# A hybrid MLA and RWKV-7 layer on one core: chunk decay factors by way of DRAM, a sum of squares in another place, down sums in another order

## What is computed

```python
def step(S, inp):
    r_t, w_t, k_t, v_t, kk_t, a_t = inp
    sa = jnp.einsum('bhvk,bhk->bhv', S, -kk_t)
    S = (S * w_t[:, :, None, :] + sa[..., None] * (kk_t * a_t)[:, :, None, :]
         + v_t[..., None] * k_t[:, :, None, :])
    return S, jnp.einsum('bhvk,bhk->bhv', S, r_t)
```

## Time and profile before

| | us |
|---|---|
| median of 3 runs | 1897.72 |
| lowest and highest | 1897.05, 1898.7 |
| the profiled execution, its time | 1898.8 |
| the profiled execution, its span in the profile | 1897.0 |
| PE busy (share of the span) | 1795.9 (95%) |
| DVE, POOL, ACT busy | 955.3, 691.5, 384.9 |
| mean granted clock of TensorE (1 is full speed) | 0.976 |

### The profile page before, as it was taken

How to read it: one execution, slowest core, us unless ns; L and a number is a source line. 1 busy time by engine, 2 the same in 40 slices (tenths; PEclk the granted TensorE clock), 3 DMA queues, 4 the chain that set the end, 5 groups by cost and what they waited for, 6 DMA issues and landing times. The chain is left out here.

```text
span 1897.0 us, 34197 instructions
## 1 busy us (share of the span) xinstructions
PE 1795.9 (95%) x14597; PEld 1336.5 (70%) x14597; DVE 955.3 (50%) x1710; ACT 384.9 (20%) x918; POOL 691.5 (36%) x495
## 2 busy tenths in 40 slices
PE   5999999999997987999899899999999999899998
PEld 3566666666665664555566788888888888688887
DVE  2757767766776773555333543343444334324422
ACT  2333333334333322333100111100001000000000
POOL 2553664555354534445320111222222220534522
PEclk9999999999997888999999999999999999999999
DMA  9343244324221006110130211101111112233331
GB/s 377 111 152 103 77 136 135 94 88 157 92 80 54 7 7 163 46 45 1 75 128 9 105 45 45 35 32 45 45 45 45 45 45 73 84 114 115 122 101 64
DMA packets 70906, 158.62 MB, mean 84 GB/s; under 512 B 19290, under 2 KB 47786, under 8 KB 66531
## 3 DMA queue, kind: packets, MB, share of 16 engines
q1 hardware_dynamic: 66866, 115.74, 19.0%
q10 hardware_dynamic: 3888, 40.70, 6.0%
HBM read 128.30 MB, written 20.44 MB: 78 GB/s over the span
## 5 line engine op out<-in xcount | busy, mean ns | idle before, releaser
L2337 PE MATMUL psum<-mixT,wA 128*128 128x264 f32 x1408 | 337.3, 388 | 1.9 <-DVE rb L2579 1.5
L2337 PEld LDWEIGHTS psum<-mixT,wA 128*128 128x128 f32 x1408 | 268.3, 191 | 48.6 <-DVE rb L2579 1.7
L2337 PE MATMUL psum<-u_sum,wA 128*128 128x264 f32 x1232 | 297.4, 386 | 0.5 <-DVE u_sum L2562 0.5
L437 PE MATMUL psum<-wsl,xt 128*128 128x368 f32 (+1 forms) x1092 | 283.8, 452 | 8.8 <-DMA wsl<-in_w_in 5.7
L2337 PEld LDWEIGHTS psum<-u_sum,wA 128*128 128x128 f32 x1232 | 234.3, 190 | 41.1 <-issue 0.9
L437 PEld LDWEIGHTS psum<-wsl,xt 128*128 128x128 f32 (+1 forms) x1092 | 150.0, 172 | 90.8 <-issue 18.1
L2492 POOL TENSOR_TENSOR wA<-wA 128x512 f32<-128x512 f32 x22 | 28.6, 1299 | 427.6 <-DMA wA<-in_w_gate 233.4
L2337 PE MATMUL psum<-hid,wA 128*128 128x264 f32 x528 | 121.6, 386 | 2.1 <-DVE hid L2630 1.5
L2337 PEld LDWEIGHTS psum<-hid,wA 128*128 128x128 f32 x528 | 100.2, 190 | 19.9 <-issue 2.8
L2505 POOL TENSOR_TENSOR u_sum<-wA 128x1280 f32<-128x1280 f32 x8 | 24.7, 3092 | 184.6 <-DMA wA<-in_w_down 184.6
L2337 PE MATMUL psum<-mixT,u_sum 128*128 128x264 f32 x352 | 82.9, 392 | 9.4 <-POOL u_sum L2511 9.4
(11 more groups left out here) (362 smaller groups left out, 2875.9 us busy)
## 6 DMA issues: line engine op xcount, KB each, us to landing
wsl<-in_w_in ACTq DMA_DIRECT2D x27, 1472.0 KB, 6.9
wA<-in_w_down SPq DMA_DIRECT2D x32, 704.0 KB, 4.1
wA<-in_w_gate SPq DMA_DIRECT2D x22, 512.0 KB, 4.4
wA<-in_w_up SPq DMA_DIRECT2D x22, 512.0 KB, 4.4
mixed<-proj SPq DMA_DIRECT2D x8, 784.0 KB
xt<-in_x_tiles SPq DMA_DIRECT2D x9, 512.0 KB, 6.0
wsl<-in_w_in SPq DMA_DIRECT2D x3, 1472.0 KB, 11.3
out_y<-hid SPq DMA_DIRECT2D x1, 4224.0 KB, 12.0
```

What stands on the lines that cost most here:

```text
L437: return pe.matmul(out, lhsT, rhs, start=start, stop=stop)
L2337: ins = pe.matmul(pb[bank][:, 0:NW], left(k), right(k), start=first and k == 0, stop=k == depth - 1, skip_group_check=not first)
```

## The change

Three parts.

1. The four products of two columns are gone, and with them ACT's exponential of `ends` and the wait for `qts_ok` ahead of them. The exponential of the running sum is now written to `grown`, which is the buffer of `sig`; POOL's product with it goes to rR. Rows 63 and 127 of `grown` are the factors of the two chunks. SP stores these two rows (2 x 2 KB) to spare rows of the scratch tensor `v` in DRAM, at the end of a step, after a wait for `rR_e`; at the start of the next step it waits for that store (`pc_st`) and loads them into `pc`, 128 x 8, of single elements of 4 bytes with channels on the partitions (`pc_in`). `pc` now has column 4c + j. `state_out` waits for `pc_in`, and the next tile's first write to `sig` waits for `pc_st` and for POOL's `R_ok`. `transposes_x` waits for `kts_ok` and `qts_ok` itself.
2. On PE `ssq(t+3)` goes behind `state_close(t,1)`, on DVE `row_mean(t+3)` behind `state_out(t,1)`.
3. In the down products POOL forms S3 first, then S2 = A22 - S3, then S1 = S2 + A11, and waits for `a22_in` only ahead of S2. DVE forms T3, T2 = T3 + B11, T1 = B22 - T2. PE runs Z ahead of Y and W. SP's waits follow the new last readers.

```diff
@@ -172,6 +172,7 @@
     keff = sb("keff", [P, RW])
+    grown = sig
     rR = sb("rR", [P, RW])
@@ -255,6 +256,7 @@
     v_rows = io.v.rearrange("t p h d -> (t p) h d")
+    ends = io.v.rearrange("t p h d -> (t p) (h d)")[KEYS:KEYS + 2 * TILES]
     ident = c_("ident")
@@ -318,7 +320,7 @@
     def decay_sums(f):
-        return (pb[4], pb[6]) if f else (pb[1], pb[2])
+        return pb[4] if f else pb[1]
 
@@ -383,6 +385,12 @@
             f = t + 1
+            if t >= 0:
+                sp.wait_ge(s["pc_st"], 16 * f)
+                if t >= 2:
+                    sp.wait_ge(s["S_ok"], 2 * t - 2)
+                sp.dma_start(pc[t % 2][:, :], ends[2 * t:2 * t + 2].rearrange("c (j p) -> p (c j)", p=P),
+                             allow_slow_non_contiguous=True).then_inc(s["pc_in"], 16)
             if f < TILES:
@@ -415,6 +423,8 @@
                     sp.dma_start(io.qT[:, :, (f - 1) * P:f * P], qts).then_inc(s["st_kv"], 16)
+                sp.wait_ge(s["rR_e"], f + 1)
+                sp.dma_start(ends[2 * f:2 * f + 2], grown[CHUNK - 1::CHUNK, :]).then_inc(s["pc_st"], 16)
 
@@ -554,24 +564,18 @@
                 return
-            inc, ends = decay_sums(f)
+            inc = decay_sums(f)
             pe.wait_ge(s["sig_ok"], f + 1)
...
                 pe.wait_ge(s["kts_ok"], f + 1)
-            mm(inc[:, :], c_("cum_inc"), sig[:, :])
-            if f:
-                pe.wait_ge(s["qts_ok"], f + 1)
-            for j in range(4):
-                last = mm(ends[:, 2 * j:2 * j + 2], sig[:, j * P:(j + 1) * P], c_("chunk"))
-            last.then_inc(s["cum_ps"], 1)
+            mm(inc[:, :], c_("cum_inc"), sig[:, :]).then_inc(s["cum_ps"], 1)
 
...
                 return
-            pe.wait_ge(s["pc_ok"], f + 1)
-            if f == 0:
-                pe.wait_ge(s["kts_ok"], 1)
-                pe.wait_ge(s["qts_ok"], 1)
+            pe.wait_ge(s["rR_e"], f + 1)
+            pe.wait_ge(s["kts_ok"], f + 1)
+            pe.wait_ge(s["qts_ok"], f + 1)
             for kind, (buf, ok) in enumerate(((aA[f % 2], "A_ok"), (rR, "R_ok"), (aB[f % 2], "B_ok"), (kK[f % 2], "K_ok"))):
@@ -921,9 +925,9 @@
             F(2)
-            ssq(t + 3, F)
             sample_keys(t, 13)
             state_close(t, 1)
+            ssq(t + 3, F)
             transposes_x(f)
@@ -1076,10 +1080,10 @@
             act.wait_ge(s["cum_ps"], f + 1)
-            inc, ends = decay_sums(f)
+            inc = decay_sums(f)
             act.activation(kK[f % 2][:, :], inc[:, :], ACT.Exp, scale=-1.0).then_inc(s["kK_e"], 1)
-            act.activation(rR[:, :], inc[:, :], ACT.Exp).then_inc(s["rR_e"], 1)
-            act.activation(pc[f % 2][:, :], ends[:, 0:8], ACT.Exp).then_inc(s["pc_ok"], 1)
+            act.wait_ge(s["eA_ok"], f + 1)
+            act.activation(grown[:, :], inc[:, :], ACT.Exp).then_inc(s["rR_e"], 1)
 
@@ -1329,7 +1333,7 @@
             pool.wait_ge(s["A_ok"], f + 1)
-            tt(rR[:, :], rR[:, :], mixed[f % 2][:, r_cols], ALU.mult).then_inc(s["R_ok"], 1)
+            tt(rR[:, :], grown[:, :], mixed[f % 2][:, r_cols], ALU.mult).then_inc(s["R_ok"], 1)
 
@@ -1489,6 +1493,9 @@
             z, a = low_rank(f)
+            if f:
+                dve.wait_ge(s["R_ok"], f)
+                dve.wait_ge(s["pc_st"], 16 * f)
             named(tt(sig[:, :], z[:, :], v_("w0"), ALU.add), "z_ok", f + 1)
@@ -1561,7 +1568,7 @@
             dve.wait_ge(s["kA_ok"], f + 1)
-            named(tt(aA[f % 2][:, :], aA[f % 2][:, :], rR[:, :], ALU.mult), "A_ok", f + 1)
+            named(tt(aA[f % 2][:, :], aA[f % 2][:, :], grown[:, :], ALU.mult), "A_ok", f + 1)
 
@@ -1630,7 +1637,8 @@
             run(tt(S[:, :, :], S[:, :, :], pb[3][:, c * 256:(c + 1) * 256].rearrange("p (j n) -> p j n", j=4), ALU.add))
-            kept = pc[t % 2][:, :].rearrange("p (j c) -> p c j", c=2)[:, c]
+            dve.wait_ge(s["pc_in"], 16 * t + 16)
+            kept = pc[t % 2][:, 4 * c:4 * c + 4]
             named(tt(S[:, :, :], S[:, :, :], bcast(kept, 2, CHUNK), ALU.mult), "S_ok", n)
@@ -1786,9 +1794,9 @@
             decayed_bk(f)
-            row_mean(t + 3)
             sample_scores(t, 13)
             state_out(t, 1)
+            row_mean(t + 3)
             bonus_sum(f)
@@ -2264,17 +2272,18 @@
                 sp.wait_ge(s["e3_ok"], n)
-                sp.wait_ge(s["e2_ok"], n)
+                sp.wait_ge(s["e1_ok"], n)
             sp.dma_start(Alo[:, 0:FH], rows(j)[:, 0:FH]).then_inc(s["a11_in"], 16)
...
                 sp.wait_ge(s["q7_ps"], n)
+                sp.wait_ge(s["e2_ok"], n)
             sp.dma_start(Ahi[:, 0:FH], rows(j + KH)[:, 0:FH]).then_inc(s["a21_in"], 16)
...
                 sp.wait_ge(s["q4_ps"], n)
-                sp.wait_ge(s["e1_ok"], n)
+                sp.wait_ge(s["e2_ok"], n)
             sp.dma_start(Ahi[:, FH:], rows(j + KH)[:, FH:]).then_inc(s["a22_in"], 16)
@@ -2413,16 +2422,18 @@
                 x_close()
+            pe.wait_ge(s["e3_ok"], n + 1)
+            pe.wait_ge(s["f3_ok"], nh + 1)
+            if n >= 2:
+                pe.wait_ge(s["q_z"], n - 1)
+            product(Z, left(Ahi[:, 0:FH]), lo1, FH, "q7_ps")
             pe.wait_ge(s["e2_ok"], n + 1)
...
             product(Y, left(S2d), lambda k: T2d[:, k, :], FH, "q6_ps")
-            pe.wait_ge(s["e3_ok"], n + 1)
-            pe.wait_ge(s["f3_ok"], nh + 1)
-            if n >= 2:
-                pe.wait_ge(s["q_z"], n - 1)
-            product(Z, left(Ahi[:, 0:FH]), lo1, FH, "q7_ps")
+            pe.wait_ge(s["e1_ok"], n + 1)
+            pe.wait_ge(s["f1_ok"], nh + 1)
             if n >= 2:
@@ -2499,19 +2510,18 @@
             pool.wait_ge(s["a21_in"], 16 * n + 16)
+            tt(Ahi[:, 0:FH], Alo[:, 0:FH], Ahi[:, 0:FH], ALU.subtract).then_inc(s["e3_ok"], 1)
             pool.wait_ge(s["a22_in"], 16 * n + 16)
+            pool.wait_ge(s["e3_ok"], n + 1)
+            if n:
+                pool.wait_ge(s["q6_ps"], n)
+            tt(S2d, Ahi[:, FH:], Ahi[:, 0:FH], ALU.subtract).then_inc(s["e2_ok"], 1)
+            pool.wait_ge(s["e2_ok"], n + 1)
             if n:
                 pool.wait_ge(s["q5_ps"], n)
-            tt(S1d[0], Ahi[:, 0:10], Ahi[:, FH:FH + 10], ALU.add)
-            tt(S1d[1], Ahi[:, 10:FH], Ahi[:, FH + 10:], ALU.add).then_inc(s["e1_ok"], 1)
-            pool.wait_ge(s["e1_ok"], n + 1)
-            if n:
-                pool.wait_ge(s["q6_ps"], n)
-            tt(S2d[:, 0:10], S1d[0], Alo[:, 0:10], ALU.subtract)
-            tt(S2d[:, 10:], S1d[1], Alo[:, 10:FH], ALU.subtract).then_inc(s["e2_ok"], 1)
-            tt(Ahi[:, 0:FH], Alo[:, 0:FH], Ahi[:, 0:FH], ALU.subtract).then_inc(s["e3_ok"], 1)
+            tt(S1d[0], S2d[:, 0:10], Alo[:, 0:10], ALU.add)
+            tt(S1d[1], S2d[:, 10:], Alo[:, 10:FH], ALU.add).then_inc(s["e1_ok"], 1)
             pool.wait_ge(s["a12_in"], 16 * n + 16)
-            pool.wait_ge(s["e2_ok"], n + 1)
             if n:
@@ -2639,9 +2649,9 @@
                     dve.wait_ge(s["q5_ps"], KH)
-                named(tt(T1d, B12, B11, ALU.subtract), "f1_ok", nh + 1)
-                named(tt(T2d, B22, T1d, ALU.subtract), "f2_ok", nh + 1)
-                tt(B12, B22, B12, ALU.subtract).then_inc(s["f3_ok"], 1)
+                named(tt(B12, B22, B12, ALU.subtract), "f3_ok", nh + 1)
+                named(tt(T2d, B12, B11, ALU.add), "f2_ok", nh + 1)
+                tt(T1d, B22, T2d, ALU.subtract).then_inc(s["f1_ok"], 1)
                 if nh:
```

More of the change, by code:

```diff
@@ L265, in layer_inputs @@
         z_ok az_ok z_e a_e sig_ok a_ok up_ps sqk_ok sqq_ok v_ok kr96_ok gate_ok st24_ms st24_ok k96_ok q96_ok kT_ps qT_ps kts_ok qts_ok
-        kkr_ok kksq_ok n8_ms n8_ok kk_ok kka_ok keff_ok rk_ok bon_ok cum_ps rR_e kK_e eA_ok kA_ok pc_ok R_ok A_ok B_ok K_ok
+        kkr_ok kksq_ok n8_ms n8_ok kk_ok kka_ok keff_ok rk_ok bon_ok cum_ps rR_e kK_e eA_ok kA_ok pc_st pc_in R_ok A_ok B_ok K_ok
         XT_ps XT_act XT_dve G1_ps G2_ps Lraw_ok E_ok D_ok GBm_ok GKm_ok Ls_ok T1_ps T1_ok ED_ps GKV_ps GKV_ok AT_ps AT_ok W_ps W_ok
```

## The result

The changed kernel takes 1876.45 us, median of 4 runs (1874.0 to 1878.91), against 1898.21 us for the kernel before (4 runs): a ratio of 0.9885 (95% interval 0.987 to 0.99), or 21.8 us less. The forecast was 1882.2 us with a range from 1877 to 1889.

What follows compares the result with a forecast made beforehand. PE was taken to bound the kernel. Parts 1, 2 and 3 gave 2.2 + 4.0 + 9.3 = 15.5 us off the profiled 1898.8 us, so 1883.3, or 1882.2 against the median; range 1877 to 1889.

Steps and rivals of the forecast that it cites:

- What bounds it: Whole kernel: PE, busy 1795.9 of 1897.0 us, so gains come only from its own list or its gaps.
- Part 1, tiles 1 to 6, 0 us: Dropping PE's small products gains 0 there, since PE then waits as long for DVE's state update; bounds 0 and 0.92 a tile.
- The first rival: State update does not hold PE in tiles 1 to 6: 6 x 0.9 us more gain, 1876.8 us; chance 0.08.
- Tile 7, 0.7: Without the small products PE goes on once the shorter state multiplication is done: gain 0.7 us, bounds 0 and 0.9.
- tile 8, 1.5: Last tile's small products take 1.64 us at a low clock and the state is ready: gain 1.5 us, bounds 0 and 1.6.
- The transfer: SP's store and single-element load of the chunk factors stay hidden, the load under 18 us: cost 0.
- the budget of 18.3 us: Time the single-element load has on SP's queue before DVE waits for shifted rows; each further us costs 8 us.
- Part 2, 0.66 x 6 = 4.0: Moving the sum of squares behind the state's close removes PE's 0.66 us idle wait for ACT in six iterations: 4.0 us.
- Part 3, first down product, 7.6: With the sums reordered, W at n = 0 starts at 1627.4 instead of 1635.04: gain 7.6 us.
- so POOL's S3 takes the turn to 1614.4: At n = 0, POOL's S3 runs behind DVE's T2, which ends at 1611.2, and takes 3.15 us.
- Part 3, the others, 1.7: From n = 1 on, PE's other two waits for down sums go: 9.4 - 7.7 = 1.7 us.
- for things done half an iteration before: DVE's added waits ahead of the next `sig` are for work already finished, so they were given no cost.

Runs made afterwards that it cites:

- part 1 alone: Kernel before with only the small products replaced by chunk decay factors by way of DRAM: 1893.0 us against 1897.73, ratio 0.9976.
- S3 behind T2: Changed kernel with POOL, at the first down product, starting S3 only when DVE's T2 has ended: 1877.38 us.
- bonus first: Changed kernel with POOL's bonus of a tile put ahead of its square of the tile after next: 1879.07 us.
- part 3 alone: Kernel before with only the down sums reordered to S3, S2, S1 and T3, T2, T1: 1887.19 us, ratio 0.9943.
- the idle waits: Kernel before with only three more DVE waits, for things long done: 1898.43 us against 1898.26; repeated, 1899.44 us, ratio 1.0002.
- the second execution: Changed kernel run again without any edit: 1875.7 us, ratio 0.9875.
- half of the edit: Changed kernel with one filler piece ahead of PE's second state step, DVE's row sum not moved: 1875.43 us; with it moved too, 1872.01.

## Why the prediction was right or wrong

- **What bounds it**: right. The gain came from PE's gaps and from PE's own small products. But one of the gaps, the one behind L8, is set by DVE and POOL, and the sum had nothing for it (last point).
- **Part 1, tiles 1 to 6, 0 us**: right, by six waits of 0.73 to 0.76 us, and part 1 alone. The first rival (the small products count in full) fell, though its time, 1876.8, is by luck the one nearest the result.
- **Tile 7, 0.7, and tile 8, 1.5**: right: 0.76 in part 1 alone, and 14.6 to 13.1 from S8 to K8. In three traces with part 1 (part 1 alone, S3 behind T2, bonus first) the gain at tile 8 is 1.9 to 2.0, so the last half microsecond there changes from one execution to the next.
- **The transfer**: right. A load of 1024 single elements landed 2.2 to 2.4 us after its issue in the changed kernel (2.1 to 2.6 in all traces with one load a tile), and the budget of 18.3 us was 19.6. The trace has 9394 DMA packets more than before, and nine loads with one packet for each of 1024 elements make 9216 of them. The Trainium skill ("DMA: Bandwidth & Descriptors", Rules for kernel authors) says that a load whose last dimension is strided becomes one descriptor per element. The packets agree, but the load is so short that it stays hidden.
- **Part 2, 0.66 x 6 = 4.0**: mechanism right, term too small; it measured 4.95. The step that failed is "gain 0.66 x 6", the reading of a bracket as the whole gap. The iteration fell from 66.93 to 66.10, 0.83 us: from `state_in` to the transposes PE took 5.87 before and 5.07 after. The bracket is the idle time behind a modelled end; the distance between starts is what moves.
- **Part 3, first down product, 7.6**: mechanism right, term too small: from X to the first product behind W it took 25.54 us where it had taken 35.01, so 9.5. The step that failed is "so POOL's S3 takes the turn to 1614.4", behind T2. By my own numbers S3's quarter landed 0.2 us after T3's end, 4.7 us after its issue; in the trace it landed after 4.2 us, and S3 began 0.2 us before T3's end and went first. In the order that I assumed (part 3 alone) it gave 8.5: there S1 was ready 21.5 us after X where my sum of turns had 22.5, since the turns were shorter than I let them be (S3 ended 3.0 us behind T2 and T1 3.0 behind S3, where I had 3.2 and 3.1). A step decided by 0.2 us needed both branches in the sum.
- **Part 3, the others, 1.7**: measured 11.7 - 9.5 = 2.2. Of the three brackets of before the two behind n = 0 showed 1.5 and 0.15 us; by starts, the products behind them came 1.7 and 0.3 us later than the usual 4.9 us: again brackets for distances.
- **L8 to S8**: missing from the sum, 2.6 us. 2.1 of it come of the turns of DVE and POOL behind a start 0.36 us earlier, which the idle waits show by themselves. The other 0.5 lie ahead of that start, where PE's granted clock differs; in the second execution these are 2.1. The step that failed is that I put DVE's new waits at nothing because they are "for things done half an iteration before": they were met, and yet a start moved.

In all 0.9 + 1.9 + 0.5 + 2.6 = 5.9 of the 6.3 us; of the rest, 0.3 stand between K8 and X and are no more than what that stretch varies by. This account is that of one pair of traces; the terms of the median are not known. The range was too narrow below: I had an upper bound of 11.5 for part 3 and used its middle for the edge.

## What to carry to other kernels

Take the length of a gap from the starts of the rows around it in both states of the code, not from the idle time in the bracket. Where two engines take turns, write out both orders whenever the first turn is decided by tenths of a microsecond, and look at what stands beside an operation that takes twice its length: the state's 0.42 us cost PE 0.7 us a tile through a POOL operation that had no part in it. When a gap can't be closed, put other work in it, and move whatever comes due next along with it: 3.8 us of PE's list here, and 1.4 with half of the edit.

## What the runs showed of the hardware that was not expected

- Added waits of DVE at three places, for things long done, moved a later start on DVE from 0.48 to 0.12 us behind POOL's operation, at one place and in every trace, and so 2.1 us at the end of a stage. At the same operation of tiles 1 to 7 the distance was 0.12 us in both kernels.
- The same edit had the granted clock at 0.93 instead of 0.97 in a stretch 450 us later, in both of its traces, and lost 2.8 us there.
- A DMA of 1024 elements of 4 bytes landed about as soon (2.1 to 2.6 us) as a store of 256 KB (2.1 us).
- The same load of 704 KB landed 4.0 to 5.2 us after its issue in fourteen traces, and that decided which of two engines had the first turn.
